# Two layer blocks in sequence on one core: the down-projection sums start with an overwriting product instead of zero-tile matmuls, and two weight splits stand behind the first routing steps

## What is computed

```
def conv_glu_ffn(n, w_up, conv_w, conv_b, w_down):
    gate, up = jnp.split(n @ w_up, 2, axis=-1)
...
    return (jax.nn.silu(conv) * up) @ w_down          # D_FF = 2816 rows of w_down, D = 1024
...
def hier_moe(h, w_group, b_group, w_expert, b_expert, w_gate, w_up, w_down):
    t = h.reshape(B * S, D)
    g_prob = jax.nn.softmax((t @ w_group + b_group).astype(jnp.float32), axis=-1)
    p_sel, g_idx = lax.top_k(g_prob, 1)               # one group for each token
    e_logits = (t @ w_expert + b_expert)...           # then two of its eight experts
...
    for g in range(N_GROUPS):
        hid = jax.nn.silu(a) * b * combine[:, g, :, None]
        y = y + jnp.einsum('nef,efd->nd', hid, w_down[g])
```

## Time and profile before

| | |
|---|---|
| time, three runs | 1616.21, 1616.61, 1618.96 us; median 1616.61 |
| span of the profiled execution | 1618.9 us |
| PE / DVE / ACT busy | 95% / 70% / 57% of the span |
| mean granted TensorE clock | 0.959 of full speed |
| HBM | 334.72 MB read, mean 207 GB/s |

### The profile page before, as it was taken

The page is one execution under the profiler, slowest core; times in us unless marked ns, Lnnn a source line. Parts: engine busy times, 40 slices in busy tenths (PEclk is TensorE's granted clock), DMA queues, the critical chain, the costliest instruction groups (busy, mean ns, idle before and its releaser), DMA issues.

```text
span 1618.9 us, 23376 instructions
## 1 busy us (share of the span) xinstructions
PE 1532.1 (95%) x8148; PEld 1292.0 (80%) x8148; DVE 1139.9 (70%) x1869; ACT 928.7 (57%) x1522; POOL 32.6 (2%) x68
## 2 busy tenths in 40 slices
PE   7999999999989999989979999999899799999997
PEld 5877899997868999977768888887678678888875
DVE  6554566567686656665767889889755678888886
ACT  5432445445455545455536767676555367777764
POOL 0000000000010000010000000000000000000000
PEclk9986899999999999999989999999997899999999
DMA  8510354544413454442226989798530458898884
GB/s 323 183 52 27 131 184 179 194 188 161 174 37 114 179 202 181 181 160 104 82 102 251 353 309 357 296 363 336 221 140 21 162 195 331 322 355 314 336 331 192
DMA packets 46828, 336.77 MB, mean 208 GB/s; under 512 B 5344, under 2 KB 5472, under 8 KB 6432
## 3 DMA queue, kind: packets, MB, share of 16 engines
q1 hardware_dynamic: 46656, 335.49, 54.8%
q0 software_dynamic: 96, 0.30, 0.1%
HBM read 334.72 MB, written 1.05 MB: 207 GB/s over the span
## 4 chain that ended last, share of the span: by engine, by line
PE 86%; DVE 6%; ACT 4%; issue 2%; POOL 1%; DMA 1%; DVEq 0%; ACTq 0%; SPq 0%; POOLq 0%
PE bank L1225 23%; PE bank L1227 23%; PE bank L1226 23%; PE bank L1327 3%; DVE w_low L701 2%; PE bank L1439 2%; PE bank L1450 2%; PE bank L1337 1%; ACT w_high L347 1%; PE bank L1273 1%; PE bank L1482 1%; PE bank L1329 1%; PE bank L1284 1%; PE bank L1348 1%; PE bank L1347 1%
## 5 line engine op out<-in xcount | busy, mean ns | idle before, releaser
L701 DVE TENSOR_TENSOR w_low<-raw,w_high 128x1024 fp32r<-128x1024 f32 (+2 forms) x630 | 734.6, 1212 | 193.2 <-ACT w_high L347 190.9
L347 ACT ACTIVATE w_high<-raw 128x1024 fp32r<-128x1024 f32 (+2 forms) x630 | 623.5, 1044 | 106.2 <-PE bank L1227 69.5
L1225 PE MATMUL bank<-w_high,x_high 128*128 128x512 f32 (+1 forms) x928 | 375.9, 405 | 8.1 <-DVE rope_b L972 3.1
L1227 PE MATMUL bank<-w_high,x_low 128*128 128x512 f32 (+1 forms) x928 | 363.7, 392 | 0.0
L1226 PE MATMUL bank<-w_low,x_high 128*128 128x512 f32 (+1 forms) x928 | 361.6, 390 | 0.0
L1225 PEld LDWEIGHTS bank<-w_high,x_high 128*128 128x128 f32 x928 | 175.5, 189 | 46.8 <-issue 7.9
L1227 PEld LDWEIGHTS bank<-w_high,x_low 128*128 128x128 f32 x928 | 175.1, 189 | 38.1
L1225 PE MATMUL bank<-x_high,w_high 128*128 128x256 f32 (+1 forms) x712 | 203.2, 285 | 0.4 <-DVE rope_b L860 0.3
L1226 PEld LDWEIGHTS bank<-w_low,x_high 128*128 128x128 f32 x928 | 176.0, 190 | 34.1 <-issue 1.4
L1226 PE MATMUL bank<-x_low,w_high 128*128 128x256 f32 (+1 forms) x712 | 202.6, 285 | 0.0
L1227 PE MATMUL bank<-x_high,w_low 128*128 128x256 f32 (+1 forms) x712 | 202.5, 284 | 0.0
(11 more groups left out here) (235 smaller groups left out, 1477.3 us busy)
## 6 DMA issues: line engine op xcount, KB each, us to landing
raw<-stream SPq DMA_DIRECT2D x314, 1024.0 KB, 4.8
const_sb<-const SPq DMA_DIRECT2D x1, 2070.0 KB, 15.1
residual<-x SPq DMA_DIRECT2D x2, 512.0 KB, 4.0
final_gain<-fgain SPq DMA_DIRECT2D x2, 512.0 KB, 10.7
out<-residual SPq DMA_DIRECT2D x2, 512.0 KB, 2.6
small_sb<-small SPq DMA_DIRECT2D x1, 765.0 KB, 6.6
rope_a<-router POOLq DMA_DIRECT2D x2, 144.0 KB, 2.5
const_sb<-const SPq DMA_DIRECT2D x1, 136.0 KB, 4.3
```

The source lines that it names most:

```text
L347: nc.scalar.activation(wh[:, u, cols], raw[:, u, cols], ACT.Copy).then_inc(w_high, 1)
L701: ins = tt(wl[:, u, cols], raw[:, u, cols], wh[:, u, cols].bitcast(F32), ALU.subtract)
L1225: mm(o, ah, bh, start=start, stop=False, **kw)
L1227: return mm(o, al, bh, start=False, stop=stop, **kw)
```

## The change

On PE, `clear()` and `clear_sums()` go from the normal path (`clear_sums` stays in the branch for overflow, which these inputs do not enter, and the zero tile is still prepared). `down` and `down_sums` get an argument `first`; where it holds, the first product of each bank has `start=True`, which overwrites the bank's 512 columns. In the FFN this needs the first `down` to be another instruction than the later ones, so the loop's first turn is written out and the loop runs from 1 to 5. On DVE the two splits ahead of the routing move: one behind the group's choice, ahead of the wait for the places; one behind the whole of `route`, ahead of the wait for `comb_ready`.

```diff
@@ DVE, route(l, meanwhile)
                 one_hot(g_log, 0, 3, 4, 5, NG).then_inc(goh_ready, 1)
                 tt(A3(1, NG), g_log, wide(0, NG), ALU.subtract).then_inc(r_sub, 1)
+                split(C_LAYER[l] + C_MOE - 1 + AHEAD)
 
                 dve.wait_ge(place_done, l + 1)
@@ DVE, moe(l)
                 route(l, lambda: gathered(0))
+                split(c0 + AHEAD)
                 dve.wait_ge(comb_ready, l + 1)
@@ DVE, layer
                 low(t_layer(l, 3), xl, xh, lambda k: ps("norm2_g", l * KT + k, l * KT + k + 1))
-                plain(c0 + C_MOE - 1, 2)
                 moe(l)
@@ PE
-            def clear():
-
-                for i in range(4):
-                    for j in range(4):
-                        mm(B[i][:, j * P:(j + 1) * P], zero[:, :], zero[:, :], start=True, stop=False, skip_group_check=True)
-
-            def down(c, off, buf, last):
+            def down(c, off, buf, last, first=False):
...
-                                          False, last and k == 1, skip_group_check=True)
+                                          first and k == 0, last and k == 1, skip_group_check=True)
@@ PE, glu(l)
-                clear()
+                def turn(i, j):
+                    c = c0 + 2 + 3 * j
+                    for u in range(2):
+                        up(i * 4 + (f0 + 2 + 2 * j + u), u, c + u, i * 2)
+                    pe.wait_ge(g_low, i * 4 + (f0 + 2 * j + 2))
+                    down(c + 2, i * 2, j, False, isinstance(i, int) and j == 0)
+
                 up(f0, 0, c0, 0, (T_F0, T_F1)[l])
                 up(f0 + 1, 1, c0 + 1, 0)
-                with pe.Fori(0, (NFB - 1) // 2) as i:
+                for j in range(2):
+                    turn(0, j)
+                with pe.Fori(1, (NFB - 1) // 2) as i:
                     for j in range(2):
...
+                        turn(i, j)
@@ PE, moe(l): turn
                     up(e + 1, c, off, g, lambda: turn_hid(e))
-                    if first is not None:
-                        if first:
-                            pe.wait_ge(ys_ready, 2 * (g0 + first))
-                        clear_sums()
-                    down_sums(e, c + 2, off, last)
+                    if first:
+                        pe.wait_ge(ys_ready, 2 * (g0 + first))
+                    down_sums(e, c + 2, off, last, first is not None)
```

More of the change, by code:

```diff
@@ L1483, in turn_hid, with down_sums @@
                     ins.then_inc(m_tr, 1)
-                def down_sums(e, c, off, last):
+                def down_sums(e, c, off, last, first=False):
                     u = c % RING
@@ L1492, in down_sums @@
                             ins = product(B[half][:, :], gh[:, 0, k, 0:P], gl[:, 0, k, 0:P], wh[:, u, lo:lo + 512],
-                                          wl[:, u, lo:lo + 512], False, last and k == 1, skip_group_check=True)
+                                          wl[:, u, lo:lo + 512], first and k == 0, last and k == 1, skip_group_check=True)
                         if last and half == 0:
```

5 lines of the change are left out of this document (removed).

## The result

The changed kernel took 1601.99 us in the median of 7 runs (1598.42 to 1613.46), the kernel before 1617.20 in 7 runs beside it (1616.16 to 1623.58). The ratio is 0.9900 with a 95% interval from 0.9868 to 0.9931. Measured once more, later, it was 1601.64 (6 runs) against 1626.19 (11 runs), ratio 0.9872 (0.9836 to 0.9908). The forecast was 1599.0 with a range from 1594 to 1605: the time lies in the range, 3.0 us above the forecast. The profiled execution has a span of 1600.6 us, 18.3 less than before; the sum of the prediction was 17.6.

A forecast was written before the change was run, and what follows sets the result against it. TensorE was taken as the bound in FFN and expert stages, VectorE's order in the routing. Terms 4.3 + 4.4 + 6.7 + 2.1 + 0.1 = 17.6 us, from the median 1616.6 to 1599.0, range 1594 to 1605.

The forecast's parts named there:

- Bound and place: TensorE bounds FFN and expert stages; in the routing VectorE's order does, and moving splits gains 4.3 and 4.4 us.
- The waits foreseen: VectorE ahead of `hidden`: it still waits for `silu`, by 4.9 us in the first layer and 2.3 in the second.
- The cost is 0 to 0.1 us: First moved split, 2.3 us, in VectorE's 2.31 us wait for the places: hole and work are the same size.
- Experts' zero tiles: Expert stages: eight groups of 8 matmuls at 0.84 us leave the chain, gain 6.7 us, each stage 3.4 us shorter.
- Transfers behind the moved splits: Two chunk loads in each MoE layer move with the splits; price 0 unless a landing took over 9 us.
- FFN's zero tiles: Start of each FFN: gain 2.1 us in the first, 0.1 in the second, as `up` waits for `x_low` anyway.
- The written-out turn: FFN loop's first turn as straight code: same matmuls and waits as the loop's turn, priced at 0.
- More than the sum: Routing: clock doesn't fall or rises sooner, saving up to some 6 us more, 1593 us; chance 0.12.
- The clock, against: Second FFN's first `up` starts at half clock, each routing loses 2.4 us; about 7 us back, 1606; chance 0.08.
- The stream takes it back: Expert stages: loads set the pace, the 6.7 us become waits for `w_low`, 1605.7 us; chance 0.07.
- The routing doesn't shorten: Routing: moved splits only move the wait, behind L910 and `hidden`; 1607.7 us; chance 0.03.
- slower: Both FFN: entering the written-out turn makes TensorE wait for instructions, 12 us each, 1623 us; chance 0.02.

The follow-up runs named there:

- half split: Changed kernel with the first moved split cut in two, its second half put behind the selection tiles; 1598.31 us, ratio 0.9878 to the kernel before; again 1604.36 us.
- added products: The half split with 12 products that nobody reads in TensorE's routing pauses; 1607.86 us, ratio 0.9893 to the kernel before, and 1595.99 us, ratio 0.9845.

## Why the prediction held, and where it was off

**Bound and place: right, shown.** Taking two splits from ahead of the bias moved the transposes to 0.57 us behind the products, and this alone gave A to C 4.4 and 4.6 us less; predicted 4.3 and 4.4. The split left no idle time ahead of the places' instruction, and `hidden` still waited. The waits foreseen were 4.9 and 2.3 us; they are 2.3 and 4.6, the larger one now in the layer in which the clock fell twice.

**"The cost is 0 to 0.1 us": right against before, but not the least that could be had.** The prediction matched a hole of 2.31 us to a split of 2.3. At full clock the place products ended 826.85, 1.25 us after the choice of the group (L905, to 825.60), and the split ended last. It said that this would cost nothing against the state before, which holds; the half split shows the 0.9 us per layer that it leaves.

**Experts' zero tiles: right.** 3.4 us per layer foreseen, 3.2 to 3.4 measured over 24 layers, 7.1 at equal clock for 6.7, both for the tiles by themselves. Nothing of the 0.05 us for the product behind is seen.

**Transfers behind the moved splits, "Price 0": not borne out in the second layer.** The stage there is 1.1 to 2.6 us above the shortest in all five profiles with moved splits and no added products, and 0 to 0.8 in the five with the splits where they were. In the first layer the price was 0. How the moved splits would do this no run shows.

**FFN's zero tiles: the term that was mis-sized.** "Gain 2.1" in the first FFN was worked out for a start at half clock in one profile, with the clock left as it was from there on. It measured 4.6 in the two profiles. In the other profiles it is 0.1 at full clock, and that by the turn's form, and some 3.2 where both starts are at half. Over its 12 runs the kernel with this part alone is 0.8 us faster at equal clock, ratio 0.9996. A term that hangs on the clock of one profile should have been given both values. For the second FFN 0.1 was right.

**The written-out turn, 0: right**, 0.0 at equal clock.

**The rivals.** *More than the sum*, by a clock that doesn't fall in the routing: it did not come about, the clock still fell in every routing profiled of the changed kernel. Nor do the runs show a gain of up to 6 us in it. With added products one routing ran at full clock throughout and took 21.3 us, as the half split's did with 3.4 us at half clock. What has a price that the traces show is the second fall. The rival had been right that ScalarE's work would take part back: it is what stands ahead of `hidden`. *The clock, against*: the place it named, the second FFN's start, was at full clock in both profiles of the changed kernel, and where an FFN did start at half clock without tiles the FFN was 3.2 us shorter, not longer. But its other half, a second fall in the routing, is real: it costs 3.3 to 3.5 us, and strikes before as after. *The stream takes it back*: one wait for `w_low` of 1.5 us appeared, which the prediction had put down as a sign against it. The whole 6.7 us were not taken back, but 1.7 and 0.7 us of them were in the changed kernel's two profiles. With only the experts' tiles gone nothing was, so it goes with the moved splits and not with the missing tiles, from which the rival had it. *The routing doesn't shorten* and *slower*: out.

**Working from one profile to a median.** The prediction subtracted its 17.6 us from the median of three runs. A run's time is in fact 1.7 us above its span, so the profiled execution, 1618.9, is a run of about 1620.6, and was not among the three. From 1620.6 the sum gives 1603.0; the profiled run of the changed kernel took 1602.31. From the median it gives 1599.0, for 1601.99. For the profiled pair the sum was right to a microsecond, and that is partly luck: the FFN gave 2.5 us more than its term, since only one of the two profiles has the start at half clock, the second layer's experts gave 1.8 less, and the second fall changed layers and so nearly cancelled. Within the groups of runs the change gave 14.3 to 15.5, some 2 to 3 less than the sum. The FFN's term, worth 0.1 in place of 2.1 wherever the clock is full, and the second layer's experts would explain that, but the runs without a profile cannot show it.

## What to carry to other kernels

Ahead of a chain that crosses engines, look for work on the waiting engine that the chain doesn't need, and put it into the holes further down; measure each hole at the clock that it will have afterwards, and cut the work smaller than the hole (here half a split let the gather start 0.9 us earlier than a whole one). A bank that is cleared only so that all products can accumulate can be overwritten by its first product, which saves the clearing wherever TensorE is the bound (here 0.84 us for eight tiles) and nothing where it waits anyway. Work moved out of a wait also moves the loads behind it: look at the stages that follow, not only at the hole. Where runs fall in groups with the granted clock, compare within a group or along the clock; the ratio of 12 runs did not show a part of 7 us that the trace and the clock line both show.

## What the runs showed of the hardware that was not expected

- The same program ran in two groups of times, about 11 us apart, with some runs between them. In the one pair of profiles where the difference was traced, most of it arises in the first attention: a stretch at half clock of 44.4 or 47.8 us in nine profiles and of 71.7 us in three, while by the profile TensorE was busy for 76 of the 78 us between 90 and 168 us.
- In the routing the clock fell, rose and fell again, for 6.8 us, in 8 of 20 cases, with 20.3 us from C to D in place of 16.6 to 17.7. The Trainium skill, "TensorE: Matmul & The Clock Gate", section "The HAM clock gate", says that the number of matmuls that run throttled varies from run to run of one kernel, with the phase of the gate when the kernel starts. These traces agree that it varies: the half split fell twice in the second layer in one profile and in the first in the other. No run here shows the phase.
- 32 matmuls with zeros in both operands, 7.07 us of TensorE without a pause, ran at a half clock that had begun 1.3 us ahead of them and lasted 2 us beyond them; in the same kernel's second FFN as many ran at full clock. Twelve products spread over the routing's pauses went with half-clock stretches of at most 3.4 us, where the first stretch was 3.4 or 6.8 without them and 10.2 with the longer pause.
- The 8 matmuls that cleared two banks cost 0.84 us in the chain and 0.81 us by the difference of 24 expert stages (3.24 us for four groups), while the 16 of an FFN at full clock cost nothing.
